# Moving a small-vector series to GpSimd and reordering the projection stage of a two-layer decoder step

## The reference, cut to what matters

```python
h = rms_norm(x, lp['attn_norm'])
z = h @ lp['w_in']          # columns: xr | cq | ckv | kpe | u | v | g
xc = conv_b + sum(xpad[:, k:k + t] * conv_w[k] for k in range(4))
r = sigmoid(einsum(xb, wa) + ba);  i = sigmoid(einsum(xb, wx) + bx)
log_a = -8.0 * r * softplus(-lam)          # lam: one number per channel
q = rms_norm(cq, ...) @ w_uq               # 6 tiles of 128 rows
latent = rms_norm(ckv, ...);  k_pe = rope(rms_norm(kpe, ...), pos)
v = gelu(v);  u = gelu(u)
```

## Time and profile before

| | |
|---|---|
| median of 3 runs | 1638.24 us (1635.48 to 1643.93) |
| the profiled execution | 1629.91 us, its span 1628.2 us, so 1.7 us lie around the span |
| PE busy | 1571.0 us, 96% of the span |
| PE's weight loads | 1518.5 us, 93% |
| DVE, ACT, POOL busy | 66%, 54%, 32% |
| granted clock of PE | 0.999 |
| HBM read, written | 228.98 MB, 2.46 MB, mean 142 GB/s |

### The profile page before, as it was taken

One profiled execution on the slowest core, in us unless ns is written; L12 is line 12 of the kernel. 1 busy time (PEld: TensorE's weight loads), 2 busy tenths in 40 slices (PEclk: granted clock), 3 DMA queues, 4 the chain that ended last, 5 costly groups with the idle time before them and its releaser, 6 DMA issues. The chain is left out here.

```text
span 1628.2 us, 33224 instructions
## 1 busy us (share of the span) xinstructions
PE 1571.0 (96%) x10860; PEld 1518.5 (93%) x10860; DVE 1069.9 (66%) x1667; ACT 885.7 (54%) x1612; POOL 521.1 (32%) x619
## 2 busy tenths in 40 slices
PE   7998999999999999999989989999999999999999
PEld 6876999999899999999988779999998999999999
DVE  6576767777555776664385867677775657666633
ACT  5586666766534454443356766766675334444432
POOL 4622367777520010000055323677765100000000
PEclk9999999999999999999999999999999999999999
DMA  7322365554454454444453214555535444444443
GB/s 260 112 78 69 116 191 153 164 155 129 147 152 144 146 154 153 143 154 147 150 180 124 84 40 135 184 155 160 161 114 182 130 144 155 145 153 143 153 147 118
DMA packets 114499, 232.90 MB, mean 143 GB/s; under 512 B 12882, under 2 KB 78483, under 8 KB 114259
## 3 DMA queue, kind: packets, MB, share of 16 engines
q1 hardware_dynamic: 111890, 222.94, 43.9%
q0 software_dynamic: 2496, 8.55, 1.5%
HBM read 228.98 MB, written 2.46 MB: 142 GB/s over the span
## 5 line engine op out<-in xcount | busy, mean ns | idle before, releaser
L1720 DVE TENSOR_TENSOR w_lo<-raw,w_hi 128x1024 fp32r<-128x1024 f32 x258 | 317.8, 1233 | 231.0 <-ACT w_hi L1270 228.4
L1270 ACT ACTIVATE w_hi<-raw 128x1024 fp32r<-128x1024 f32 x258 | 272.2, 1057 | 344.4 <-PE PS L779 333.2
L779 PE MATMUL PS<-h_hi,w_hi 128*128 128x320 f32 x1360 | 426.2, 313 | 16.7 <-DVE h_lo L1772 10.4
L779 PE MATMUL PS<-h_hi,w_lo 128*128 128x320 f32 x1360 | 421.8, 310 | 0.0
L779 PE MATMUL PS<-h_lo,w_hi 128*128 128x320 f32 x1360 | 421.7, 310 | 0.0
L779 PEld LDWEIGHTS PS<-h_hi,w_hi 128*128 128x128 f32 x1360 | 256.8, 189 | 21.1 <-issue 12.4
L779 PEld LDWEIGHTS PS<-h_lo,w_hi 128*128 128x128 f32 x1360 | 256.9, 189 | 0.6
L779 PEld LDWEIGHTS PS<-h_hi,w_lo 128*128 128x128 f32 x1360 | 256.7, 189 | 0.0
L1270 ACT ACTIVATE ksqp<-PS 128x512 f32<-128x512 f32 x256 | 153.2, 598 | 159.8 <-PE PS L1020 157.6
L1020 PE MATMUL PS<-comb_hi,lt_hi 128*128 128x288 f32 x1024 | 239.9, 315 | 0.0
L2095 DVE TENSOR_REDUCE kss<-ksqp 128x8 f32<-128x512 f32 x256 | 174.3, 682 | 98.8 <-ACT ksqp L1270 97.9
(11 more groups left out here) (317 smaller groups left out, 2670.9 us busy)
## 6 DMA issues: line engine op xcount, KB each, us to landing
raw<-in_stream SPq DMA_DIRECT2D x258, 512.0 KB, 3.5
tpage<-in_tcache SPq DMA_DIRECT2D x256, 192.0 KB, 2.5
rrow<-in_rcache SPq DMA_DIRECT2D x256, 128.0 KB, 2.5
x<-in_xT SPq DMA_DIRECT2D x2, 640.0 KB, 5.6
sbias<-in_sbias POOLq DMA_DIRECT2D x2, 640.0 KB, 7.2
out_yT<-x SPq DMA_DIRECT2D x4, 320.0 KB, 2.2
const<-in_consts SPq DMA_DIRECT2D x1, 1088.0 KB
wgate<-in_wgate POOLq DMA_DIRECT2D x2, 512.0 KB, 4.0
```

Of the source, the lines that this page charges most:

```text
L779: done = mm(out, w[:, slot, c], a, start=first and n == 0 and m == 0, stop=last and n == len(pairs) - 1 and m == 2)
L1270: return nc.scalar.activation(out, in_, func, **kw)
L1720: V.tensor_tensor(w_lo[:, s, :], raw[:, s, :], f(w_hi[:, s, :]), ALU.subtract).then_inc(lo_done.sem, 1)
```

## The change

Seven things are done, in each layer unless said otherwise. (1) Series: DVE keeps an addition and a reciprocal (`lru_reciprocal`); the rest of the series, 25 instructions with 21 drains, runs on POOL behind the six weight DMAs and ahead of the sampled convolution. (2) `vec` is loaded by SP: in layer 0 between the first weight unit and x, for layer 1 in the middle of the weight stream, where the loop over units is cut in two. (3) `norm_sums` goes behind unit 3, and unit 4 goes to bank 7 instead of bank 0. (4) Unit 10 goes ahead of the latent and key sums. (5) The eight `wgate` products are spread: j = 0 behind unit 11, j = 1 behind 12, j = 2 behind 13, j = 3 behind 14; ACT's tanh follow the same pattern between its query tiles, and ACT's square of va goes behind the first two tanh, ahead of split 15. (6) DVE gates `ti` behind split 16 and the rotated key instead of ahead of split 15. (7) At the start of layer 1 DVE updates two tiles of x ahead of its split of unit 0, and ACT splits unit 1 behind tile 5 instead of behind tile 7.

```diff
@@ -432,6 +432,7 @@
...
+        sp.dma_start(vec[:], ins["vecs"][0]).then_inc(vec_in.sem, 16)
@@ -534,7 +535,12 @@
...
-            stream(l, 10, groups - 3)
+            half = U_G // SLOTS - 1
+            stream(l, 10, half - 10)
+            if l + 1 < DEPTH:
+                sp.wait_ge(h_ready.sem, h_ready.at(l + 1, 0))
+                sp.dma_start(vec[:], ins["vecs"][l + 1]).then_inc(vec_in.sem, 16)
+            stream(l, half, groups - 3 - (half - 10))
@@ -552,11 +558,33 @@
...
+        def softplus(l):
+            e, s, q, p = (sm(c, 0, 4) for c in (S_E, S_S, S_Q, S_P))
+            g = nc.gpsimd
+            pool.wait_ge(par_abs.sem, par_abs.at(l, 2))
+            pool.sem_inc(waits_passed, 1)
+            g.memset(p, 1.0 / 17.0)
+            g.tensor_tensor(s, s, e, ALU.mult)
+            pool.drain()
+            g.tensor_tensor(q, s, s, ALU.mult)
+            pool.drain()
+            for odd in (15, 13, 11, 9, 7, 5, 3, 1):
+                g.tensor_tensor(p, p, q, ALU.mult)
+                pool.drain()
+                g.tensor_scalar(p, p, 1.0 / odd, None, ALU.add)
+                pool.drain()
+            g.tensor_tensor(p, p, s, ALU.mult)
+            g.tensor_scalar(q, v("lam", 0, 4), -1.0, 0.0, ALU.mult, ALU.max)
+            pool.drain()
+            g.tensor_scalar(p, p, 2.0, None, ALU.mult)
+            pool.drain()
+            g.tensor_tensor(q, p, q, ALU.add)
+            pool.drain()
+            g.tensor_scalar(sm(S_SP4, 0, 4), q, 4.0, None, ALU.mult)
+            g.tensor_scalar(sm(S_NSP4, 0, 4), q, -4.0, None, ALU.mult).then_inc(params.sem, 1)
+
...
-            pool.wait_ge(h_ready.sem, h_ready.at(l, 0))
-            pool.sem_inc(waits_passed, 1)
-            pool.dma_start(vec[:], ins["vecs"][bass.ds(l, 1)].rearrange("o p n -> p (o n)")).then_inc(vec_in.sem, 16)
@@ -575,6 +603,7 @@
...
+            softplus(l)
@@ -810,13 +839,13 @@
...
             full_unit(l, 2, 2, 2)
+            full_unit(l, 3, 0, 3)
             norm_sums(l)
-            full_unit(l, 3, 0, 3)
-            full_unit(l, 4, 1, 0)
+            full_unit(l, 4, 1, 7)
             pe.wait_ge(bank_free[5].sem, banks.take(l, 5))
...
             grouped(PS[:, 5, 0:T], ones[:], [tmp8[:, i, :] for i in (0, 1)]).then_inc(cstat.sem, 1)
-            for u, bank in ((5, 1), (6, 2), (7, 3), (8, 0), (9, 1)):
+            for u, bank in ((5, 1), (6, 2), (7, 3), (8, 0), (9, 1), (10, 2)):
                 full_unit(l, u, u % SLOTS, bank)
@@ -825,17 +854,20 @@
...
             mm(PS[:, 7, 0:T], cst("blk32"), tmp8[:, 4, :], start=True, stop=True).then_inc(cstat.sem, 1)
-            for u, bank in ((10, 2), (11, 3), (12, 0)):
-                full_unit(l, u, u % SLOTS, bank)
-
-            pe.wait_ge(small_in.sem, small_in.at(l, 64))
-            for j in range(4):
+
+            def recurrence_gates(j):
                 pe.wait_ge(conv_done.sem, conv_done.at(l, j + 1))
...
                     mm(PS[:, b, 0:T], wgate[:, g, j, :], xc[:, j, :], start=True, stop=True).then_inc(lgate_mm.sem, 1)
+
+            full_unit(l, 11, 11 % SLOTS, 3)
+            pe.wait_ge(small_in.sem, small_in.at(l, 64))
+            recurrence_gates(0)
+            full_unit(l, 12, 12 % SLOTS, 0)
+            recurrence_gates(1)
 
@@ -844,6 +876,7 @@
...
                     last.then_inc((unit_done if m == len(ms) - 1 else uq_mm).sem, 1)
+                recurrence_gates(2 + u - 13)
             pe.wait_ge(bank_free[4].sem, banks.take(l, 4))
@@ -1312,12 +1345,11 @@
...
             else:
-                for m in range(KT - 1):
+                for m in range(KT):
                     tile_hi(l, m)
                     tile_square(l, m)
-                tile_hi(l, KT - 1)
-                split(l, 1)
-                tile_square(l, KT - 1)
+                    if m == KT - 3:
+                        split(l, 1)
             split(l, 2)
@@ -1373,23 +1405,14 @@
...
             root(rt[:, 0, :]).then_inc(crs.sem, 1)
-            split(l, 13)
-            act.wait_ge(cscaled.sem, cscaled.at(l, 2))
-            A(lat_hi[:], lat[:], ACT.Copy).then_inc(chi.sem, 1)
-            split(l, 14)
-
-            act.wait_ge(z_scaled.sem, z_scaled.at(l, 13))
-            A(ge[:], va[:], ACT.Square).then_inc(gsq.sem, 1)
-
-            act.wait_ge(params.sem, params.at(l, 1))
-            for j in range(4):
+            def recurrence_tanh(j):
                 for g, dst, hb in ((0, tr, S_HBA), (1, ti, S_HBX)):
...
                     release(b)
-            split(l, 15)
-            for m, bank in ((0, 1), (1, 2), (2, 3), (3, 0)):
+
+            def query_tile(m, bank):
                 if m < 3:
@@ -1398,6 +1421,23 @@
...
                 release(bank)
+
+            split(l, 13)
+            act.wait_ge(cscaled.sem, cscaled.at(l, 2))
+            A(lat_hi[:], lat[:], ACT.Copy).then_inc(chi.sem, 1)
+            split(l, 14)
+            act.wait_ge(params.sem, params.at(l, 1))
+            recurrence_tanh(0)
+            act.wait_ge(z_scaled.sem, z_scaled.at(l, 13))
+            A(ge[:], va[:], ACT.Square).then_inc(gsq.sem, 1)
+            split(l, 15)
+            recurrence_tanh(1)
+            query_tile(0, 1)
+            query_tile(1, 2)
+            recurrence_tanh(2)
+            query_tile(2, 3)
+            query_tile(3, 0)
+            recurrence_tanh(3)
             split(l, 16)
@@ -1736,36 +1776,11 @@
...
-        def lru_softplus_start(l):
+        def lru_reciprocal(l):
...
-            s, q, p = sm(S_S, 0, 4), sm(S_Q, 0, 4), sm(S_P, 0, 4)
-            V.tensor_scalar_add(s, sm(S_E, 0, 4), 2.0)
+            V.tensor_scalar_add(sm(S_S, 0, 4), sm(S_E, 0, 4), 2.0)
...
-            V.reciprocal(s, s)
-            dve.drain()
-            V.tensor_tensor(s, s, sm(S_E, 0, 4), ALU.mult)
-            dve.drain()
-            V.tensor_tensor(q, s, s, ALU.mult)
...
-            dve.drain()
-            V.tensor_scalar_mul(sm(S_SP4, 0, 4), q, 4.0)
-            V.tensor_scalar_mul(sm(S_NSP4, 0, 4), q, -4.0).then_inc(params.sem, 1)
+            V.reciprocal(sm(S_S, 0, 4), sm(S_S, 0, 4)).then_inc(par_abs.sem, 1)
@@ -1803,13 +1818,9 @@
...
 
-            lru_softplus_start(l)
-            lru_softplus_terms((15, 13, 11))
+            lru_reciprocal(l)
             split(l, 3)
-            lru_softplus_terms((9, 7, 5))
             split(l, 4)
-            lru_softplus_terms((3, 1))
-            lru_softplus_end(l)
             dve.wait_ge(rb_ready.sem, rb_ready.at(l, 1))
@@ -1819,7 +1830,7 @@
...
             split(l, 7)
-            scaled_rows(l, 4, 0)
+            scaled_rows(l, 4, 7)
             conv(1)
@@ -1853,12 +1864,9 @@
...
             scaled(l, 12, 0, va[:, 3, :])
-
-            dve.wait_ge(lgate.sem, lgate.at(l, 8))
-            V.scalar_tensor_tensor(ti[:], ti[:], 1.0, xc[:], ALU.add, ALU.mult).then_inc(lru_gated.sem, 1)
             split(l, 15)
+
             split(l, 16)
-
             dve.wait_ge(consts_in.sem, 32)
@@ -1866,6 +1874,9 @@
...
             V.tensor_tensor(kpe[:], kpe[:], rt[:, 1, :], ALU.add).then_inc(kpe_ready.sem, 1)
+            dve.wait_ge(lgate.sem, lgate.at(l, 8))
+            V.scalar_tensor_tensor(ti[:], ti[:], 1.0, xc[:], ALU.add, ALU.mult).then_inc(lru_gated.sem, 1)
+
             dve.wait_ge(gth.sem, gth.at(l, 1))
@@ -2262,9 +2273,6 @@
...
             more = l + 1 < DEPTH
-            if more:
-                split(l + 1, 0)
-                dve.wait_ge(vec_in.sem, vec_in.at(l + 1, 16))
             for m in range(KT):
@@ -2272,6 +2280,9 @@
...
                 release(m)
+                if more and m == 1:
+                    split(l + 1, 0)
+                    dve.wait_ge(vec_in.sem, vec_in.at(l + 1, 16))
                 if more and m:
```

More of the change, by code:

```diff
@@ L63 @@
                           ("cos", T), ("sin", T), ("mask", 384), ("fold", 128)))
-BANK_USES = [36, 36, 35, 34, 12, 17, 16, 9]
+BANK_USES = [35, 36, 35, 34, 12, 17, 16, 10]
 def build_program(nc, ins, outs):
@@ L252, in build_program @@
     par_exp = Signal("lru_exp", 1)
-    par_abs = Signal("lru_abs", 1)
+    par_abs = Signal("lru_abs_and_reciprocal", 2)
     params = Signal("lru_params", 1)
@@ L1737, in lru_parameters @@
             V.tensor_tensor(sm(S_GQK), v("qn_g"), v("kn_g"), ALU.mult)
-        def lru_softplus_start(l):
+        def lru_reciprocal(l):
             dve.wait_ge(par_exp.sem, par_exp.at(l, 1))
-            s, q, p = sm(S_S, 0, 4), sm(S_Q, 0, 4), sm(S_P, 0, 4)
-            V.tensor_scalar_add(s, sm(S_E, 0, 4), 2.0)
+            V.tensor_scalar_add(sm(S_S, 0, 4), sm(S_E, 0, 4), 2.0)
             dve.drain()
-            V.reciprocal(s, s)
-            dve.drain()
-            V.tensor_tensor(s, s, sm(S_E, 0, 4), ALU.mult)
-            dve.drain()
-            V.tensor_tensor(q, s, s, ALU.mult)
-            V.memset(p, 1.0 / 17.0)
-            dve.drain()
-        def lru_softplus_terms(odds):
-            q, p = sm(S_Q, 0, 4), sm(S_P, 0, 4)
-            for odd in odds:
-                V.tensor_tensor(p, p, q, ALU.mult)
-                dve.drain()
```

(12 more changed lines are left out.)

## The result

| | before | after |
|---|---|---|
| first set of runs, median | 1636.20 us (1634.28 to 1643.93, 7 runs) | 1621.21 us (1616.12 to 1629.91, 7 runs) |
| ratio, first set | | 0.9908, 95% interval 0.9889 to 0.9927 |
| two more sets, ratio | | 0.9934 (0.9911 to 0.9957) and 0.9917 (0.9895 to 0.9939) |
| mean granted clock, all sets | 0.9922 over 91 runs | 0.9951 over 19 runs |
| the profiled execution | 1629.91, clock 0.999 | 1621.21, span 1619.4, clock 0.996 |

By the medians of the three sets the kernel is faster by 13 to 15 us. No run of either kernel was in the slow state, so all runs are compared. The 91 runs of before are those taken beside the experiments and as one of them; the first set of seven has no clock on record. The page of after, its first part, beside the earlier trace rows: the shares have moved by one point at most, so the page alone tells nothing of where the time went.

What follows compares the result with a forecast made beforehand. PE bounds the kernel overall; in the projection stage what counts is when ACT reaches split 16. Gains of 1.9 + 3.9 + 4.3 = 10.1 off 1638.24 give 1628.1 us, range 1622 to 1635 for 8 in 10.

Steps and rivals of the forecast that it cites:

- The sum: Whole kernel: gains of 1.9 at the start, 3.9 in layer 0 and 4.3 in layer 1 make 10.1 us.
- Rivals A to D: Half absorbed, 0.20; DVE contention eats gain, 0.08; POOL becomes the bound, slower, 0.05; nothing changes, 0.05 (in letter order).
- The start: Layer 0's start: with `vec` from SP, ACT's first tile begins at 6.4 instead of 8.30, gaining 1.9 us.
- Series, norm's sum, bank 7: Projection, units 3 and 4: PE's waits of 1.13 and 1.14 go, 2.27 us; `rb` is there at 28.0.
- the margin at unit 5: DVE has unit 5's `w_lo` at 31.3, PE wants it at 31.8: 0.5 us to spare.
- The series on POOL: POOL behind the last weight DMA: 25 instructions take 14 us (11 at nearest row, 36 at most), hidden.
- Hidden, with 13 us over: POOL's sampled convolution, pushed to 41 to 59, still meets PE's and ACT's needs with 13 us reserve.
- Rival C: POOL becomes the bound from about 1.0 us per instruction; kernel 8 us slower, 1646; chance 0.05.
- rival B: Contention on DVE, from POOL's instructions, loses 3 us a layer, leaving a gain of 4: 1634; chance 0.08.
- Unit 10, the spread, the square: Layer 0 up to split 16: waits of 0.85 and 2.84 go, ACT's wait is filled; split 16 3.9 us earlier.
- DVE's clamp: DVE's clamp may be held up by POOL's split of the key weights, costing up to 1 us.
- Layer 1: Layer 1's projection: the same 3.9 plus 0.55 of the 1.52 wait ahead of unit 1; 4.3 us taken.

Runs made afterwards that it cites:

- The longer series: The changed kernel with 16 more small instructions and drains on POOL, results unused: median 1637.29 us, ratio 0.9994.
- before's second profile: Profiled execution of the kernel before, run again unaltered as the one measured: median 1637.79 us, ratio 1.0001.

## Why the prediction was right or wrong, point by point

The forecast was a gain of 10.1 and 1628.1 us; measured were 1621.2 in the first set, 1625.4 and 1623.0 in the two others, 1623.5 over all 19 runs. The mean gain over all runs is 13.8 us, of which 9.8 (0.6 either way) remains at equal clock and 3.9 goes with the clock; with the flattest and the steepest slope of a single set, 0.9 and 1.6 us per 0.001, 9.8 would be 11.2 and 9.1.

**The step that failed** is "The sum", 1.9 + 3.9 + 4.3 = 10.1: it adds removed idle time only and has no term for PE's granted clock, which it takes as the same in both kernels. The runs showed a mean clock of 0.9951 in place of 0.9922, worth 3.9 us. The profile that the sum was made on ran at 0.999 and had no low stretch behind any of the waits that the change removes. The row that could have told is the 8.3 us by which that execution lay under the median; I carried it over unchanged instead of asking what made it. What makes the clock higher stays open (see above). The sentence "What lies behind the projection ... is untouched and moves along" is not refuted: from the first query tile of layer 0 to PE's first product of layer 1 the two profiles of before took 737.5 and 736.5 us, the three of after 738.3, 740.4 and 741.2. Of this the profiles of before spent 3.4 and 0 us at the 0.50 level, those of after 6.8, 10.2 and 10.2.

The three terms are also somewhat small by the marks. From PE's first product of a layer to the first query tile behind split 16 it is 70.70 and 71.50 us in before's first profile, 66.36 and 66.01 in after's, none of these with low clock behind the first unit: 4.3 and 5.5 where 3.9 and 4.3 were forecast. With 1.7 for the start that is 11.6, against 9.8 at equal clock; the record does not decide between the two.

Luck had a hand. The first set of after fell on high clocks (0.9957), and its 1621.2 lies under the range of 1622 to 1635; the median of all 19 runs lies inside it. That POOL's long pause did no harm was luck too, as the pause used 10 of the 13 us that were taken to be over. The range allowed for a gain of 16, but for the scatter of the runs and not for a difference of the clock between the kernels. Rivals A to D, all on the side of less gain, were wrong; more gain through the clock was not among them.

**The start.** 1.9 forecast, 2.5 and 2.6 measured by one edit alone and undone. The mechanism holds (`vec` 3.4 us from SP, no longer the releaser), but the estimate of x pushed back by 0.3 said nothing on x's own scatter: 5.4 to 7.6 us in its landing (middle of the two halves), so ACT's first tile hits the forecast 6.4 within 0.3 in four profiles of ten. `vec` took 6.3 to 6.7 us from POOL's queue and 3.2 to 3.7 from SP's. The estimate of 2.2 us by the fit of the Trainium skill (DMA: Bandwidth & Descriptors, Anatomy of one DMA), which is for a DMA issued by GpSimd, is not borne out on that queue here.

**Series, norm's sum, bank 7.** Right: both waits went (0.24 is left of the first), and the margin at unit 5 held. `rb` was there at 26.6, where 28.0 less the 1.9 of the start makes 26.1. First matmul of the latent's sums at 51.17 without a wait. A detail was off: each removed wait should give its idle time and some 0.16 more, an estimate from the records, where matmuls without a gap overlap by that much (0.31 long, 0.147 apart).

**The series on POOL.** Wrong in size: 14 (11 to 18) forecast, 23.3 measured, 10 of it the pause. "Hidden, with 13 us over" was in truth 2.9 and 2.1. The trace of before could have told of the pause (3.05 us at 36.67). The per-instruction price of 0.46 was near (0.36 alone, 1.2 to 1.3 beside a split). The 1.44 beside a split was compared with 0.32, the time of an addition; it is a multiplication, and one alone takes 0.4 to 0.5 (0.49 at 39.38 in before). Rival C's threshold was stated in the price of an instruction; the pause was not in sight, and it used three quarters of the reserve. The longer series showed what lies behind it.

**Contention (rival B).** Wrong for after, right for the mirror image: with the series on DVE it is POOL's additions that stretch it, 0.80 for 0.16. POOL's product beside DVE's split took 1.17 for 0.20. The lock that the Trainium skill (SBUF — State Buffer, SBUF: two separate sides) describes, held for a whole instruction by whichever of the two starts first, agrees with these rows in both directions.

**Unit 10, the spread, the square.** Right in these marks: split 16 at 73.33 against 73.6 forecast, 0.67 left of the wait for unit 12 against 0.5, new waits of 1.24 and 1.14 against 1.5 and 1.3. Undone, the spread costs 2.9 at equal clock and 6.7 by the marks; alone it gives 4.0 and 5.1.

**DVE's clamp** took more than "up to 1": 2.35 beside POOL's split of the key weights where it had been 0.83, and nothing waited for it before PE's next need:

```profile
81.83 2.35 DVE L1884 TENSOR_SCALAR mu<-mu 128x1280 f32<-128x1280 f32 x1 [1.78 <-ACT tr L1303]
```

**Layer 1.** 4.3 forecast, 5.5 found between the two profiled executions: PE's first product of the layer came 5.2 us earlier than before, split 16 10.7 earlier. PE's unit 1 waits 1.09 less where 0.55 was taken; the other 0.7 was not traced.

**Do the parts add up?** Undone one by one, `vec` 2.6, series 4.4 and spread 2.9 are 9.9 at equal clock, where the whole is worth 9.8; each is good to about 1, and unit 10, unit 4's bank and the order at layer 1's start were not undone by themselves. In raw means the three are 6.2, 8.4 and 7.5, together 22 where the whole is 13.8: each kernel with one part undone is back at before's clock (0.9924, 0.9921, 0.9917), so the share of the clock is not a sum over the parts.

## What to carry to other kernels

A wait of PE costs its idle time and sometimes a stretch of low clock behind it, so before a wait is priced, look at the granted clock behind it in more than one execution, and give more gain than forecast a rival of its own. When work is moved to POOL, count what stands around it in the queue (here a pause of 6 to 10 us at the first drain behind a group of DMAs), not only its instructions, and test the reserve by adding work. Read an experiment in raw time, at equal clock and by marks of the trace: where the three disagree, as here by up to 6 us, the price of a part is not known better than that.

## What the runs showed of the hardware that was not expected

- TensorE's granted clock, averaged over an execution, ran from 0.984 to 1.000 in one kernel or another; 0.001 of it is 0.9 to 1.6 us of these 1.6 ms. It falls in stretches at the 0.50 level, in before's second profile of 3.4 us each in the projection stage and of up to 10.2 further on; those of the projection stage, in all fourteen profiles, stood in or directly behind idle times of PE, between 1.52 and 7.00 us long, and the same idle time had one in some executions and none in others.
- POOL stood still for 10.08 and 8.36 us (layers 0 and 1) at its first drain behind six DMA issues, with no releaser; with the series moved ahead, for 6.83 and 7.79, again at the first drain behind them. In all fourteen profiles such a pause ended 0.79 to 0.92 us after the last packet of POOL's own transfers.
- 96 KB took 6.3 to 6.7 us from POOL's queue and 3.2 to 3.7 from SP's, at the same place in the program.
- DVE's 128x4 product took 0.16 alone and 0.80 beside a POOL addition; POOL's took 0.20 alone and 1.17 beside a DVE split.
